# GpSimd takes three of the eight tiles of the residual update at two norm boundaries

## The chip, the cores and the metric

One core of one Trainium2 chip runs the whole program. The metric is the device time in microseconds, median over runs. The engines are named as in the profile: PE is TensorE, DVE is VectorE, ACT is ScalarE, POOL is GpSimd and SP is SyncE.

## The reference

Two hybrid transformer layers run one behind the other on 256 positions of 1024 features. The part that matters here is the end of the mixer and the end of the feed-forward block in the first layer:

```
x = x + gt1 * rmsnorm(mix, mix_post_g)
h = rmsnorm(x, ffn_pre_g) * (1.0 + sc2) + sh2
...
x = x + gt2 * rmsnorm(f, ffn_post_g)
h = rms_norm(x, attn_norm_2) * (1.0 + scale_a) + shift_a     # layer two
```

Here rmsnorm(v, g) is v * rsqrt(mean(v * v) + 1e-6) * g, the mean going over the 1024 features. So each boundary holds two norms in a row: one over the block's output, and, once x is updated, one over x.

## The kernel before

Features lie on the partitions: X is 128 x 8 x 256, eight tiles of 128 features by 256 positions, all float32. Linear layers run on TensorE as three products of high and low parts. ScalarE copies each weight chunk of 128 x 1024 from `ring` to its high part `WH` and GpSimd subtracts it from the original to get the low part `WL` (L505; the helper `low`, called by `lows` for a range of chunks). There are four slots, and a chunk's split waits until ScalarE has done the high part, which waits until the slot is free. Each engine has one instruction queue, in an order written out by hand, and semaphores tie the queues together.

A boundary goes like this. The last linear layer of the block leaves eight tiles in PSUM. ScalarE writes each to MIX (first boundary) or FO (second), scaled by gain and gate (L1414), and squares it (L1413). VectorE adds up the squares, TensorE sums them over the partitions, and `stat_root` on ScalarE makes the inverse root, RS[:, 0, :] (L1144, L1146; a table load stands between the two activations). Then `add_normed` on VectorE updates X: in three pairs of tiles and two single ones it multiplies the source by RS (L2052, 512 or 256 columns) into a slot of CT, waits for that with `st.link`, and adds it to X (L2053), which counts up `x_ready`. `square_x` on ScalarE waits for those counts and squares X into SQ (L1430) by the list SPANS, which counts up `sq_ready`. TensorE sums the eight squares with a matrix of ones as they come (`stat`), ScalarE makes the second inverse root, RS[:, 1, :], and `make_h` on VectorE with `make_hh` on ScalarE gives the high and low parts of h (L1791, L1187, L1796), tile by tile. TensorE's next linear layer begins with the first tile of h. While TensorE waits it runs `fill`: short products whose result is not used, ahead of each wait.

X is updated twice more in layer two, on VectorE alone (L2407), and SP stores it at the end. All wait on counts of `x_ready`.

GpSimd's queue is one call of `lows` from the middle of the first layer to the projection `o2` of the second; before it stand 16 products of the first layer's branch (L532).

Of the kernel before, what the change touches and what calls it, by code (L numbers as in the profile page):

```python
# [14 lines left out]
P = 128  # L15
T = 256
D = 1024
KD = D // P
FF = 2816
KF = FF // P  # L20
# [15 lines left out]
SLOTS = 4  # L36
# [46 lines left out]
PLAN = Stream()  # L83
# [33 lines left out]
SCRATCH = {}  # L117
# [9 lines left out]

OUT_Y, OUT_NSA, OUT_MLA = 0, 16, 24
SQ_O1, SQ_DOWN1 = 5, 21

ADA_AT = {}
for _n in range(8):
# [11 lines left out]
PAIR_END = PAIR_Q + HEADS1 // 2  # L144
# [27 lines left out]
def build(nc, x_t, par_in, ada_w, wts, out_t):  # L172
    F32, F32R, BF16 = mybir.dt.float32, mybir.dt.float32r, mybir.dt.bfloat16
    ALU, ACT, AX = mybir.AluOpType, mybir.ActivationFunctionType, mybir.AxisListType
    MUL, ADD, SUB = ALU.mult, ALU.add, ALU.subtract
    ctx = ExitStack()
    with ctx:
# [3 lines left out]
        def sem(name):  # L181
            return ctx.enter_context(nc.semaphore(name))
# [12 lines left out]
        X = sb("X", [P, KD, T])  # L195
# [9 lines left out]
        RS = sb("RS", [P, 2, T])  # L205
# [49 lines left out]
        MIX = region(R, 4096, a=8, b=T)  # L255

        FAH, FAL = region(RR, 0, a=KF, b=T), region(RR, KF * T, a=KF, b=T)
        FO = region(R, 12288, a=8, b=T)
# [58 lines left out]
        rs_ready = sem("rs_ready")  # L317
# [6 lines left out]
        fall_ready = sem("fall_ready")  # L324
        diff_ready, decay_ready, m_ready, m_used = sem("diff"), sem("decay"), sem("m_ready"), sem("m_used")
        y_ready, yn_ready, mixin_ready = sem("y_ready"), sem("yn_ready"), sem("mixin_ready")
        x_ready = sem("x_ready")
        lead_ready, evac_done = sem("lead_ready"), sem("evac_done")
        t_ready, hh_ready = sem("t_ready"), sem("hh_ready")
        wdt_hi, wdt_ready = sem("wdt_hi"), sem("wdt_ready")  # L330
# [3 lines left out]
        f_begun, f_conv, f_silu, f_act = sem("f_begun"), sem("f_conv"), sem("f_silu"), sem("f_act")  # L334
# [55 lines left out]
        def _(sp):  # L390
# [81 lines left out]
            uq, ukv, o2 = (PLAN.at[name][0] for name in ("uq", "ukv", "o2"))  # L472
            assert ukv + 4 == o2
            while c < CHUNKS:
# [4 lines left out]
                n = 0  # L479
# [10 lines left out]
                    load(c)  # L490
                    c += 1
            for j in range(KD):
                sp.wait_ge(x_ready, 3 * KD + j + 1)
                sp.dma_start(out_t[:, j * T:(j + 1) * T], X[:, j, :]).then_inc(out_sem, 16)
            sp.wait_ge(out_sem, 16 * KD)

# [1 line left out]
        @block.gpsimd  # L498
        def _(pool):
            def low(q, i=0):  # L500

                pool.wait_ge(hi_done, q + 1 + i * SLOTS)
                n = PLAN.cols[PLAN.chunk_of[q]]
                k = q % SLOTS
                nc.gpsimd.tensor_tensor(WL[:, k, 0:n], ring[:, k, 0:n], WH[:, k, 0:n].bitcast(F32), SUB  # L505
                                        ).then_inc(lo_done, 1)

            def lows(q, last):

                while q < last:  # L510
                    n = 0
                    while q + n < last and PLAN.cols[PLAN.chunk_of[q + n]] == PLAN.cols[PLAN.chunk_of[q]]:
                        n += 1
                    rounds = n // SLOTS
                    if rounds >= 2:
                        with pool.Fori(0, rounds, 1) as i:
                            for k in range(SLOTS):
                                low(q + k, i)
                        q += rounds * SLOTS
                    else:  # L520
                        low(q)
                        q += 1

            G = nc.gpsimd
            st = Steps(pool, pool_step)

            lows(0, PAIR_Q)

            for j in range(HEADS1 // 2):
                n = OUT_Y + j  # L530
                pool.wait_ge(o_free[n % 2], n // 2 + 1)
                G.tensor_tensor(Z[:, j, :], XBC[:, j, :], Z[:, j, :], MUL).then_inc(y_ready, 1)  # L532
            pool.wait_ge(lo_done, PAIR_END)
            lows(PAIR_END, PLAN.q("o2"))


            pool.wait_ge(mla_sq, 1)
            pool.wait_ge(cp_ready, 1)
            pool.wait_ge(kb_ready, 1)
            for t in range(2):  # L540
                k3 = KB[:, t, :].rearrange("p (h d) -> p h d", d=QK)
                rs = mlars[:, 16 * t + 8:16 * t + 16].unsqueeze(2)
                G.tensor_tensor(k3[:, :, 0:HD], k3[:, :, 0:HD], rs.to_broadcast([P, 8, HD]), MUL).then_inc(kb_scaled, 1)  # L543
                G.tensor_tensor(k3[:, :, HD:QK], KR[:, t, :].unsqueeze(1).to_broadcast([P, 8, ROPE]),
                                rs.to_broadcast([P, 8, ROPE]), MUL).then_inc(kb_scaled, 1)

            lows(PLAN.q("o2"), SPLITS)
# [3 lines left out]
        def _(pe):  # L551
# [120 lines left out]
            def stat(name, squares, n, i=0, base=None):  # L672
                out = scratch(name, i)
                for k in range(n):
                    stat_block(out, k, n, squares, base)
# [112 lines left out]
            for i in range(8):  # L788
                t, q = divmod(i, 4)
# [14 lines left out]
            for p in range(HEADS1 // 2 + 1):  # L804
                if p < HEADS1 // 2:
                    unit(PLAN.at["in1"][1] + 64 + p, PLAN.q("in1") + 64 + p, 1, h_hi, h_lo)
                if p >= 1:
                    n = p - 1
# [4 lines left out]
                    for t in range(2):  # L813
                        for e in range(2):
                            rows = slice(64 * e, 64 * e + 64)
                            cols = slice(P * n + 64 * e, P * n + 64 * e + 64)
                            m = SM[:, n % 2, 384 * e + t * 256:384 * e + t * P + 256]
# [19 lines left out]
            fill(u0, 6)  # L837
            pe.wait_ge(rs_ready, 6)
            fill(u0, 5)
            stat("stat_ffn1", sq_at, 8, base=13)  # L840
            fill(u0, 6)
            pe.wait_ge(rs_ready, 7)
            fill(u0, 4)
# [6 lines left out]
            fill(u0, 6)  # L850
            pe.wait_ge(rs_ready, 8)
            fill(u0, 5)
            stat("stat_attn", sq_at, 8, base=29)
            fill(u0, 6)
            pe.wait_ge(rs_ready, 9)
            fill(u0, 4)
# [17 lines left out]
            for c in range(1, 9):  # L874
                for t in range(2):
                    bank_wait(u0 + 2 * c + t)
                for part in range(2):
# [4 lines left out]
                    for t in range(2):  # L882
                        out = psL[:, (u0 + 2 * c + t) % 4, 0:256]
                        for b in range(4):
                            k = 4 * part + b
# [250 lines left out]
        def _(act):  # L1136
# [282 lines left out]
                    if m == 6:  # L1419
                        preload()  # L1420

            SPANS = ((0, 2), (2, 2), (4, 2), (6, 1), (7, 1))

            def square_x(base, sq_free_after):

                preload()
                act.wait_ge(s_done, sq_free_after + 1)
                for j, n in SPANS:
                    act.wait_ge(x_ready, base + j + n)
                    A(SQ[:, j * T:(j + n) * T], X[:, j:j + n, :].rearrange("p a b -> p (a b)"), ACT.Square).then_inc(sq_ready, n)  # L1430

            for n in range(2):
                act.wait_ge(s_free[n], (SCRATCH["stat_o1"] + 1 - n) // 2)
            scale_and_square("o1", MIX, lead[:, 8:16], 0, SQ_O1)
            stat_root("stat_o1", D, RS[:, 0, :])
            square_x(0, SCRATCH["stat_o1"])
            stat_root("stat_ffn1", D, RS[:, 1, :])
            make_hh(mod[:, 24:32], 8)

# [62 lines left out]
            act.wait_ge(f_act, KF)  # L1502
            scale_and_square("down1", FO, lead[:, 24:32], 1, SQ_DOWN1)
            stat_root("stat_down1", D, RS[:, 0, :])
            square_x(8, SCRATCH["stat_down1"])
            stat_root("stat_attn", D, RS[:, 1, :])
            make_hh(mod[:, 0:8], 16)
            u0 = PLAN.at["tok2"][1]
# [217 lines left out]
            def square_o2(m):  # L1726

                if m >= 1:
                    act.wait_ge(x_ready, 16 + m)
                    A(square_place(m - 1, 2), X[:, m - 1, :], ACT.Square).then_inc(sq_ready, 1)  # L1730

            act.wait_ge(s_done, SCRATCH["mla_p"] + 8)
# [19 lines left out]
        def _(dve):  # L1752
# [290 lines left out]
            def add_normed(src, rs, x_base):  # L2043

                def wide(buf, j, n):
                    return buf[:, j:j + n, :]

                for j, n, slot in ((0, 2, 0), (2, 2, 2), (4, 2, 0), (6, 1, 2), (7, 1, 3)):
                    t = CT[:, slot:slot + n, :]
                    if j >= 4:  # L2050
                        dve.wait_ge(x_ready, x_base + j - 2)
                    st.link(V.tensor_tensor(t, wide(src, j, n), rs.unsqueeze(1).to_broadcast([P, n, T]), MUL))  # L2052
                    V.tensor_tensor(wide(X, j, n), wide(X, j, n), t, ADD).then_inc(x_ready, n)  # L2053

            for m in range(8):
                add_squares(m, 5)
# [2 lines left out]
            dve.wait_ge(mixin_ready, 8)  # L2059
            dve.wait_ge(rs_ready, 6)  # L2060
            dve.wait_ge(evac_done, 8)
            add_normed(MIX, RS[:, 0, :], 0)
            dve.wait_ge(x_ready, 8)
            dve.wait_ge(rs_ready, 7)
            make_h(mod[:, 24:32], lead[:, 16:24], RS[:, 1, :], 8)

# [76 lines left out]
            dve.wait_ge(rs_ready, 8)  # L2143
            dve.wait_ge(f_act, KF)
            dve.wait_ge(evac_done, 16)
            add_normed(FO, RS[:, 0, :], 8)


            dve.wait_ge(x_ready, 16)
            dve.wait_ge(rs_ready, 9)  # L2150
            make_h(mod[:, 0:8], lead[:, 0:8], RS[:, 1, :], 16)

# [408 lines left out]
```

## Time and profile before

| | us |
|---|---|
| median of 3 runs | 1059.93 |
| lowest and highest | 1059.37, 1061.55 |
| span of the profiled execution | 1056.5 |
| median of the runs less that span | 3.4 |
| TensorE busy in it | 1025.1 (97%) |
| VectorE busy in it | 556.2 (53%) |
| ScalarE busy in it | 634.4 (60%) |
| GpSimd busy in it | 689.8 (65%) |

The span runs from the first to the last instruction of one profiled execution; the time of a run also holds what lies around it. No time of a run is given for the profiled execution itself, so the median of the runs stands beside its span. A busy share is an average over all stages, and a TensorE that runs filler products counts as busy.

### The profile page before, as it was taken

The page shows a single profiled execution, that of the slowest core. Times are in us where ns is not written, and L with a number is a line of the kernel's source. Part 1 is how long each engine was busy: PE and PEld are TensorE (multiplying, and loading weights), DVE is VectorE, ACT ScalarE, POOL GpSimd, SP SyncE. Part 2 cuts the span into 40 slices and gives each one's busy share as a digit, 9 for nine tenths or more (in the row PEclk, how much of TensorE's full clock was granted, in tenths as well). Part 3 has the DMA queues.
Part 4 walks back from the last instruction along what each step waited for, and adds up shares of the span by engine and source line. Part 5 has one row for each costly group of instructions (what it writes and reads, how often), then busy time and mean ns, then how long its engine had stood idle before and what let it go on. Part 6 is the DMA issues. An engine that isn't in the chain of part 4 may idle for free.

```text
span 1056.5 us, 23232 instructions
## 1 busy us (share of the span) xinstructions
PE 1025.1 (97%) x8537; PEld 966.4 (91%) x8537; DVE 556.2 (53%) x1165; ACT 634.4 (60%) x1133; POOL 689.8 (65%) x306
## 2 busy tenths in 40 slices
PE   7999999999999989999999899999989999999998
PEld 5999999988799979999999799998667699999998
DVE  2577625579874435565522542296566735444400
ACT  4555764477774576666645656744566557666642
POOL 2598899811269855988799287790031075988795
PEclk9999999999999999999999999999999999999999
DMA  9988888655547863777687289865201043665563
GB/s 380 383 306 282 273 307 298 235 191 187 174 146 259 282 236 105 273 235 248 204 279 268 80 283 360 330 239 191 99 21 60 1 140 122 217 193 189 168 217 111
DMA packets 62616, 226.43 MB, mean 214 GB/s; under 512 B 6960, under 2 KB 8272, under 8 KB 61264
## 3 DMA queue, kind: packets, MB, share of 16 engines
q1 hardware_dynamic: 61344, 221.23, 60.5%
q10 hardware_dynamic: 1200, 4.23, 1.4%
q8 instruction: 46, 0.75, 0.3%
q14 instruction: 26, 0.21, 0.1%
HBM read 224.35 MB, written 1.08 MB: 213 GB/s over the span
## 4 chain that ended last, share of the span: by engine, by line
PE 75%; issue 9%; POOL 9%; DVE 3%; ACT 3%; DMA 1%; POOLq 0%; ACTq 0%; DVEq 0%; SPq 0%
PE psL L553 68%; POOL WL L505 8%; PE psO L553 3%; PE psS L553 2%; PE psL L1092 1%; DMA ring<-wts 1%; ACT psL L1685 0%; ACT WH L1155 0%; ACT R L1273 0%; PE psS L1036 0%; ACT L1146 0%; DVE sm L2288 0%; PE psS L1063 0%; PE psS L966 0%; DVE CT L2052 0%
## 5 line engine op out<-in xcount | busy, mean ns | idle before, releaser
L505 POOL TENSOR_TENSOR WL<-ring,WH 128x1024 fp32r<-128x1024 f32 (+1 forms) x282 | 670.4, 2399 | 239.8 <-ACT WH L1155 186.7
L553 PE MATMUL psL<-HR,WH 128*128 128x256 f32 (+1 forms) x3096 | 513.5, 278 | 1.8 <-DVE HR L1796 0.9
L553 PEld LDWEIGHTS psL<-HR,WH 128*128 128x128 f32 (+1 forms) x3096 | 452.6, 187 | 7.5 <-issue 4.8
L553 PE MATMUL psL<-HR,WL 128*128 128x256 f32 x1536 | 396.2, 276 | 0.0
L1155 ACT ACTIVATE WH<-ring 128x1024 fp32r<-128x1024 f32 (+1 forms) x210 | 216.5, 1042 | 107.8 <-PE psL L553 71.9
L553 PEld LDWEIGHTS psL<-HR,WL 128*128 128x128 f32 x1536 | 275.2, 188 | 0.0
L553 PE MATMUL psL<-RR,WH 128*128 128x256 f32 x1356 | 205.2, 277 | 2.4 <-DVE RR L1981 1.2
L553 PEld LDWEIGHTS psL<-RR,WH 128*128 128x128 f32 x1356 | 185.5, 187 | 3.8 <-issue 2.8
L553 PE MATMUL psL<-RR,WL 128*128 128x256 f32 x672 | 145.0, 277 | 0.3 <-POOL WL L505 0.3
L2080 DVE SCALAR_TENSOR_TENSOR CT<-psL,par,CT 128x254 f32<-128x254 f32 (+1 forms) x176 | 80.9, 480 | 107.1 <-ACT CT L1463 102.0
L1454 ACT ACTIVATE WH<-ring 128x1024 fp32r<-128x1024 f32 (+1 forms) x88 | 92.9, 1058 | 71.4 <-PE psL L553 68.0
L1783 DVE SCALAR_TENSOR_TENSOR adaring<-adaring,psO 128x1024 f32<-128x1024 f32 x80 | 96.9, 1217 | 70.6 <-DMA adaring<-ada_w 66.5
L553 PEld LDWEIGHTS psL<-RR,WL 128*128 128x128 f32 x672 | 107.6, 188 | 0.6 <-POOL WL L505 0.5
L532 POOL TENSOR_TENSOR R<-R 128x256 f32<-128x256 f32 x16 | 13.4, 839 | 59.5 <-DVE R L1920 59.5
L1463 ACT ACTIVATE CT<-psL,par 128x256 f32<-128x256 f32 x88 | 48.2, 548 | 6.2 <-PE psL L553 6.2
L553 PE MATMUL psL<-WH,HR 128*128 128x256 f32 (+1 forms) x294 | 50.4, 278 | 0.7 <-DVE HR L1796 0.7
L553 PEld LDWEIGHTS psL<-WH,HR 128*128 128x128 f32 (+1 forms) x294 | 44.4, 186 | 1.0 <-issue 0.9
L1835 DVE SCALAR_TENSOR_TENSOR R<-psL,par,R 128x255 f32 (+2 forms) x72 | 34.7, 481 | 16.5 <-DVE R L1835 14.3
L543 POOL TENSOR_TENSOR R<-R,mlars 128x1024 f32<-128x1024 f32 x2 | 3.8, 1895 | 57.5 <-DVEq L2324 57.5
L2038 DVE TENSOR_TENSOR CT<-CT,psS 128x256 f32<-128x256 f32 x21 | 8.8, 421 | 60.6 <-ACT psS L1413 55.8
L553 PE MATMUL psL<-WL,HR 128*128 128x256 f32 x144 | 39.8, 276 | 0.0
L2407 DVE SCALAR_TENSOR_TENSOR X<-psL,mod,X 128x256 f32<-128x256 f32 x16 | 7.7, 484 | 59.0 <-PE psL L553 58.8
(274 smaller groups left out, 1122.8 us busy)
## 6 DMA issues: line engine op xcount, KB each, us to landing
ring<-wts SPq DMA_DIRECT2D x285, 512.0 KB, 4.2
adaring<-ada_w SPq DMA_DIRECT2D x80, 512.0 KB, 4.8
R<-ada_w SPq DMA_DIRECT2D x8, 1024.0 KB, 16.2
ring<-wts SPq DMA_DIRECT2D x16, 384.0 KB, 3.8
R<-cum_dram ACTq DMA_DIRECT2D x8, 512.0 KB, 4.1
R<-wts SPq DMA_DIRECT2D x8, 512.0 KB, 6.4
ring<-wts SPq DMA_DIRECT2D x8, 288.0 KB, 2.8
adaring<-wts SPq DMA_DIRECT2D x4, 512.0 KB, 5.2
```

What stands on the lines that cost most here:

```text
L505: nc.gpsimd.tensor_tensor(WL[:, k, 0:n], ring[:, k, 0:n], WH[:, k, 0:n].bitcast(F32), SUB).then_inc(lo_done, 1)
L532: G.tensor_tensor(Z[:, j, :], XBC[:, j, :], Z[:, j, :], MUL).then_inc(y_ready, 1)
L553: return nc.tensor.matmul(out, lhsT, rhs, start=start, stop=stop)
L1092: last = nc.tensor.transpose(out[0:wd, n * P:(n + 1) * P], src[:, t, o:o + wd], pv("ident"))
L1155: A(WH[:, k, 0:n], ring[:, k, 0:n], ACT.Copy).then_inc(hi_done, 1)
L1454: A(WH[:, q % SLOTS, 0:n], ring[:, q % SLOTS, 0:n], ACT.Copy).then_inc(hi_done, 1)
L1463: A(CT[:, 2 * slot + b, :], psL[:, u % 4, 0:T], ACT.Identity, scale=par[:, bass.ds(w0 + 2 * 44 + b * KF + j + it, 1)], bias=par[:, bass.ds ...
L1783: V.scalar_tensor_tensor(w, w, 1.0, cond, MUL, MUL, accum_out=col).then_inc(ada_used, 1)
L1835: ins = V.scalar_tensor_tensor(dst, psL[:, (u0 + k) % 4, 0:T - back], par[:, bass.ds(m + (c_w + (3 - back) * NXBC), 1)], dst, MUL, ADD)
L2038: ins = V.tensor_tensor(SUMS, SUMS, psS[:, m % 2, 0:T], ADD).then_inc(sq_added, 1)
L2080: ins = V.scalar_tensor_tensor(dst, psL[:, us[b] % 4, 0:T - back], par[:, bass.ds(w0 + (2 - back) * 44 + b * KF + j + it, 1)], dst, MUL, ADD)
L2407: V.scalar_tensor_tensor(X[:, m, :], lin(u), gates[:, m:m + 1], X[:, m, :], MUL, ADD).then_inc(lin_free[u % 4], 1)
```

## The change

`add_normed` on VectorE ends after tile 4: pairs (0, 1) and (2, 3), and tile 4 alone. GpSimd's queue gets `add_normed_tail`: tiles (6, 7) as a pair, then tile 5, each with a multiplication in place in the source tile and an addition to X that counts up the new semaphore `xpool_ready`. `square_x` takes the tiles in the order (0, 1), (6, 7), (2, 3), 4, 5, and TensorE sums the squares in that order. VectorE waits for GpSimd's tiles before it makes h. GpSimd's one call of `lows` becomes three, with a tail after the fourth chunk of `up1` and after the fourth of `tok2`. The counts of `x_ready` are named, since VectorE now counts 5 tiles and not 8 at these two boundaries.

```diff
+X_O1, X_DOWN1, X_O2, X_OUT = 0, 5, 10, 18
...
             pool.wait_ge(lo_done, PAIR_END)
-            lows(PAIR_END, PLAN.q("o2"))
+
+            def add_normed_tail(src, rs, use):
+
+                pool.wait_ge(rs_ready, 6 + 2 * use)
+                pool.wait_ge(evac_done, 8 * (use + 1))
+                for j, n in ((6, 2), (5, 1)):
+                    t, x = src[:, j:j + n, :], X[:, j:j + n, :]
+                    st.link(G.tensor_tensor(t, t, rs.unsqueeze(1).to_broadcast([P, n, T]), MUL))
+                    G.tensor_tensor(x, x, t, ADD).then_inc(xpool_ready, n)
+
+            lows(PAIR_END, PLAN.q("up1") + SLOTS)
+            pool.wait_ge(mixin_ready, 8)
+            add_normed_tail(MIX, RS[:, 0, :], 0)
+            lows(PLAN.q("up1") + SLOTS, PLAN.q("tok2") + SLOTS)
+            pool.wait_ge(f_act, KF)
+            add_normed_tail(FO, RS[:, 0, :], 1)
+            lows(PLAN.q("tok2") + SLOTS, PLAN.q("o2"))
...
-            stat("stat_ffn1", sq_at, 8, base=13)
+            stat("stat_ffn1", lambda k: sq_at((0, 1, 6, 7, 2, 3, 4, 5)[k]), 8, base=13)
...
-            stat("stat_attn", sq_at, 8, base=29)
+            stat("stat_attn", lambda k: sq_at((0, 1, 6, 7, 2, 3, 4, 5)[k]), 8, base=29)
...
-            SPANS = ((0, 2), (2, 2), (4, 2), (6, 1), (7, 1))
+            SPANS = ((0, 2, x_ready, 2), (6, 2, xpool_ready, 2), (2, 2, x_ready, 4), (4, 1, x_ready, 5), (5, 1, xpool_ready, 3))
...
-                for j, n in SPANS:
-                    act.wait_ge(x_ready, base + j + n)
+                for j, n, done_by, count in SPANS:
+                    act.wait_ge(done_by, count + (base if done_by is x_ready else 0 if base == X_O1 else 3))
...
-                for j, n, slot in ((0, 2, 0), (2, 2, 2), (4, 2, 0), (6, 1, 2), (7, 1, 3)):
+                for j, n, slot in ((0, 2, 0), (2, 2, 2), (4, 1, 0)):
...
+                dve.wait_ge(xpool_ready, 3 if x_base == X_O1 else 6)
```

## Rows read from the trace of the kernel before

**Rows 1.** The page's busy line: busy us, share of the span, instructions.
```profile
PE 1025.1 (97%) x8537; PEld 966.4 (91%) x8537; DVE 556.2 (53%) x1165; ACT 634.4 (60%) x1133; POOL 689.8 (65%) x306
```

**Rows 2.** Chain of waits, whole span: start us, us, what.
```profile
391.44 2.03 PE psS L553 x8
...
397.42 173.33 PE psL L553 x1524
...
584.95 5.39 PE psS L553 x16
```

**Rows 3.** Timeline, first boundary: start us, us, engine, line, form, idle before and releaser.
```profile
384.18 2.35 POOL L505 TENSOR_TENSOR WL<-ring,WH 128x1024 fp32r<-128x1024 f32 x1 [1.11 <-ACT WH L1155]
...
386.28 0.79 DVE L2052 TENSOR_TENSOR CT<-R,RS 128x512 f32<-128x512 f32 x1 [3.28 <-ACT RS L1146]
...
387.18 0.69 DVE L2053 TENSOR_TENSOR X<-X,CT 128x512 f32<-128x512 f32 x1
...
387.99 0.63 ACT L1430 ACTIVATE SQ<-X 128x512 f32<-128x512 f32 x1 [0.28 <-DVE X L2053]
...
388.77 1.10 PE L553 MATMUL psS<-SQ,par 128*128 128x256 f32 x4 [1.14 <-ACT SQ L1430]
...
391.83 0.42 DVE L2053 TENSOR_TENSOR X<-X,CT 128x256 f32<-128x256 f32 x1
392.30 0.42 ACT L1430 ACTIVATE SQ<-X 128x256 f32<-128x256 f32 x1 [0.38 <-DVE X L2053]
...
397.42 0.50 PE L553 MATMUL psL<-HR,WH 128*128 128x256 f32 x2 [0.50 <-DVE HR L1796]
```

**Rows 4.** Timeline, second boundary.
```profile
582.42 0.85 DVE L2052 TENSOR_TENSOR CT<-R,RS 128x512 f32<-128x512 f32 x1 [1.96 <-ACT RS L1146]
...
584.95 5.38 PE L553 MATMUL psS<-SQ,par 128*128 128x256 f32 x16 [1.13 <-ACT SQ L1430]
...
588.49 0.42 ACT L1430 ACTIVATE SQ<-X 128x256 f32<-128x256 f32 x1 [0.38 <-DVE X L2053]
```

**Rows 5.** Busy time by window: window, us; per engine; granted clock, DMA share, GB/s.
```profile
386.20:392.72 6.52, 4.89 (x24) 3.61 (x24) 5.59 (x10) 4.21 (x7) 0.33 (x1) 1.00 0.48 165
...
582.40:588.91 6.51, 5.34 (x21) 4.27 (x22) 5.65 (x10) 4.21 (x7) 0.32 (x1) 0.74 0.59 223
```

**Rows 6.** One line each: instructions, ns min/median/max, first and last start.
```profile
L2052 DVE TENSOR_TENSOR CT<-R,RS x10: 419/684/849, 386.3 to 587.6; 128x512 f32<-128x512 f32 x6, 128x256 f32<-128x256 f32 x4
...
L532 POOL TENSOR_TENSOR R<-R x16: 727/776/1645, 228.3 to 284.0; 128x256 f32<-128x256 f32 x16
...
L544 POOL TENSOR_TENSOR R<-R,mlars x2: 1042/1042/1043, 770.8 to 773.7; 128x512 f32<-128x512 f32 x2
```

**Rows 7.** Timeline, 691 to 708 us: splits and VectorE's instructions on two SBUF tiles.
```profile
691.48 2.59 POOL L505 TENSOR_TENSOR WL<-ring,WH 128x1024 fp32r<-128x1024 f32 x1
...
694.02 2.59 POOL L505 TENSOR_TENSOR WL<-ring,WH 128x1024 fp32r<-128x1024 f32 x1
694.27 2.62 DVE L2195 SCALAR_TENSOR_TENSOR R<-R,par,RS 128x256 f32<-128x256 f32 x1
...
702.46 2.85 POOL L505 TENSOR_TENSOR WL<-ring,WH 128x1024 fp32r<-128x1024 f32 x1
...
705.28 2.85 POOL L505 TENSOR_TENSOR WL<-ring,WH 128x1024 fp32r<-128x1024 f32 x1
```

**Rows 8.** Timeline, 284.5 us.
```profile
283.87 1.22 DVE L1926 TENSOR_TENSOR WL<-ring,WH 128x1024 fp32r<-128x1024 f32 x1
284.04 1.65 POOL L532 TENSOR_TENSOR R<-R 128x256 f32<-128x256 f32 x1 [0.42 <-DVE R L1920]
```

**Rows 9.** Timeline, 676 us: a split beside an instruction that reads PSUM (psO).
```profile
675.79 2.41 POOL L505 TENSOR_TENSOR WL<-ring,WH 128x1024 fp32r<-128x1024 f32 x1
...
675.92 1.22 DVE L1783 SCALAR_TENSOR_TENSOR adaring<-adaring,psO 128x1024 f32<-128x1024 f32 x1 [4.65 <-DMA adaring<-ada_w]
```

**Rows 10.** Timeline, GpSimd, 400 to 410 us.
```profile
407.08 4.78 POOL L505 TENSOR_TENSOR WL<-ring,WH 128x1024 fp32r<-128x1024 f32 x2 [20.55 <-ACT WH L1454]
```

More of the change, by code:

```diff
@@ L326, in build @@
         y_ready, yn_ready, mixin_ready = sem("y_ready"), sem("yn_ready"), sem("mixin_ready")
-        x_ready = sem("x_ready")
+        x_ready, xpool_ready = sem("x_ready"), sem("xpool_ready")
         lead_ready, evac_done = sem("lead_ready"), sem("evac_done")
@@ L492, in _ @@
             for j in range(KD):
-                sp.wait_ge(x_ready, 3 * KD + j + 1)
+                sp.wait_ge(x_ready, X_OUT + j + 1)
                 sp.dma_start(out_t[:, j * T:(j + 1) * T], X[:, j, :]).then_inc(out_sem, 16)
@@ L1435, in _ @@
             stat_root("stat_o1", D, RS[:, 0, :])
-            square_x(0, SCRATCH["stat_o1"])
+            square_x(X_O1, SCRATCH["stat_o1"])
             stat_root("stat_ffn1", D, RS[:, 1, :])
@@ L1504, in _ @@
             stat_root("stat_down1", D, RS[:, 0, :])
-            square_x(8, SCRATCH["stat_down1"])
+            square_x(X_DOWN1, SCRATCH["stat_down1"])
             stat_root("stat_attn", D, RS[:, 1, :])
@@ L1728, in square_o2 @@
                 if m >= 1:
-                    act.wait_ge(x_ready, 16 + m)
+                    act.wait_ge(x_ready, X_O2 + m)
                     A(square_place(m - 1, 2), X[:, m - 1, :], ACT.Square).then_inc(sq_ready, 1)
@@ L2061, in _ @@
             dve.wait_ge(evac_done, 8)
-            add_normed(MIX, RS[:, 0, :], 0)
-            dve.wait_ge(x_ready, 8)
+            add_normed(MIX, RS[:, 0, :], X_O1)
+            dve.wait_ge(x_ready, X_DOWN1)
             dve.wait_ge(rs_ready, 7)
@@ L2145, in _ @@
             dve.wait_ge(evac_done, 16)
-            add_normed(FO, RS[:, 0, :], 8)
-            dve.wait_ge(x_ready, 16)
+            add_normed(FO, RS[:, 0, :], X_DOWN1)
+            dve.wait_ge(x_ready, X_O2)
             dve.wait_ge(rs_ready, 9)
```

## The prediction

> **What bounds the kernel now.** I read the page's busy line first. TensorE is busy 97% of 1056.5 us and GpSimd 65% [rows 1], so GpSimd has time to give over the whole span, but a share of the span says nothing about one stage. So next the chain of waits around the two boundaries of layer one. At the first it leaves TensorE's linear products, goes through VectorE (the normed value, then X), ScalarE (squares), eight square sums on TensorE, the root on ScalarE, and comes back to the products at 397.42 [rows 2]. All of it is a serial stretch in which TensorE does only filler products. A microsecond saved or lost there moves everything behind it, because TensorE runs for 173 us without a gap from 397.42 on. The timeline of the stretch gives each link's length [rows 3], and the second boundary has the same shape 196 us later [rows 4].
>
> VectorE works from 386.28 to 391.83 + 0.42 = 392.25; the last square runs from 392.30 to 392.72 and the square sums end at 391.44 + 2.03 = 393.47, 0.75 after the last square [rows 2, 3]. At the second boundary the last square ends at 588.49 + 0.42 = 588.91, but the sums end at 584.95 + 5.39 = 590.34, 1.43 after it [rows 2, 4]. The granted TensorE clock explains the difference: 1.00 in the first stretch of updates, 0.74 in the second, so part of the second ran at 1.2 GHz and not 2.4 [rows 5]. Just before, TensorE had idled for 1.13 us ahead of its first square sum, between short groups of filler [rows 4]. That fall costs 1.43 - 0.75 = 0.68 us.
>
> **What the change removes and adds.** At each boundary VectorE keeps two pairs and one single tile, six instructions. A 512-column pair (0.68 + 0.69) and a 256-column single (2 x 0.42) go: 2.21 us [rows 3, 6]. GpSimd gets four new instructions: two of 512 columns and two of 256. If both engines ran freely beside each other, X would be complete about 1.2 us earlier (worked out as rival A). GpSimd has the time: its last weight split before the boundary ends at 384.18 + 2.35 = 386.53, and the next starts at 407.08 after 20.55 us of idleness [rows 3, 10]; after the second boundary TensorE starts its products in the same way, so I take the same gap. So the splits are delayed by nothing, the added waits on GpSimd's queue hold back no split that could run, and moving the tail between two loops of splits costs nothing. If that cover were gone, 4 us of tail would delay the weights by up to that. SP's queue sees only renamed counts. VectorE's new wait for GpSimd comes after its own last addition, where only the root was waited for anyway.
>
> **The two engines do not run freely beside each other.** Look at a stretch where GpSimd has splits queued and VectorE has instructions that read two SBUF tiles [rows 7]. A 256-column VectorE instruction takes 2.62 us in it. A 256-column addition to X takes 0.42 [rows 3]. And GpSimd's 1024-column split takes 2.59 instead of 2.35. They strictly take turns: one split, one VectorE instruction, and so on. With 256 columns between, the splits start 694.02 - 691.48 = 2.54 us apart; with 512 columns 705.28 - 702.46 = 2.82. It works the other way too: a 256-column GpSimd multiplication that began while VectorE had a 1024-column one took 1.65 us where the median is 0.776 [rows 6, 8]. And it depends on the operands: a VectorE instruction that reads one operand from PSUM takes 1.22 us with a split running beside it at 2.41, neither much delayed [rows 9]. All ten updates of X at a boundary read two SBUF tiles, and the four of GpSimd too. Even in the present kernel the very first one shows it: 0.79 (0.85 at the second boundary) where the median of its line is 0.684, because the last split was still running [rows 3, 4, 6].
>
> Now the price. From the two spacings 256 more columns cost 0.28, so VectorE holds its turn 0.28 for 256 columns and 0.56 for 512, and a 1024-column split holds it 2.54 - 0.28 = 2.26, 0.09 less than its 2.35. GpSimd's 512 columns have no row of this form. Between 0.776 for 256 and 2.35 for 1024, 256 columns are worth 0.52, so 1.30 for 512 and 0.69 for 256 when 0.09 is off each: turns of 1.21 and 0.69. The bounds are 1.04 from the one 512-column GpSimd form that the trace has, whose second operand is one repeated value [rows 6], and 1.30 plus nothing given back. I take 1.21, since these operands are like the split's.
> All turns together: VectorE 4 x 0.56 + 2 x 0.28 = 2.80, GpSimd 2 x 1.21 + 2 x 0.69 = 3.80, sum 6.60. They start at 386.39 (0.10 is lost to the last split, as now). In order: VectorE's first multiplication to 387.0; GpSimd's, waiting since 386.6, gets in while VectorE waits for its own result; then alternately. The first pair of X is complete at about 388.8 instead of 387.87 [rows 3], GpSimd's pair at 390.0, the second pair at 391.7, GpSimd's single tile at 392.4, and VectorE's single one, with 0.25 between its two instructions and after the second, at 386.39 + 6.60 + 0.25 = 393.24, where all of X was complete at 392.25. ScalarE then has two single squares to do one behind the other, where only one was left before: 393.28 to 394.02. Last square 394.02 - 392.72 = **1.30 us later**, at each boundary. Lower bound 0.68 (GpSimd's turns 0.95 and 0.64, by the shorter form and the shortest of 256 columns, 0.727), upper bound 2.4 (every instruction holds its turn for its whole duration: 3.6 + 4.1 = 7.7 instead of 6.6).
>
> The Trainium skill has a rule for this, on the page "SBUF — State Buffer", section "Who interferes with whom": a VectorE instruction with two SBUF inputs and a GpSimd instruction that reads SBUF share a port pair, and the second to start blocks until the first is wholly done. Rows 7 agree that one blocks and give a shorter turn: 2.82 for a 512-column instruction and a split, where the whole durations would be 2.35 + 0.69 = 3.04. By the rule to the letter the change would cost the upper bound, 4.8 us over both boundaries; by the rows it is 2.6.
>
> The clock comes on top. At the second boundary the square sums ended late because half of them ran at the lower clock; later squares shift them by 1.3 if the fall stays where it is, and by 1.30 - 0.68 = 0.62 if it goes. At the first boundary TensorE's idle time ahead of the first sum, 1.14 now [rows 3], grows by the 0.9 that the first pair is late. The second boundary fell at 1.13 of it in such a pattern while the first did not, so with 2.0 at both a fall is likelier: I take half of 0.68 for the first and keep the fall at the second. Sum: 1.30 + 0.34 + 1.30 = 2.94. Behind the boundaries nothing takes it back, since what follows, root, H and the products, is in the same chain. The profiled execution's span is 1056.5; the median of the runs, 1059.93, lies 3.4 above it, which I take as what lies around the span and leave alone. 1059.93 + 2.94 = **1062.9 us**.
>
> **Rivals.**
> (A) The engines do run side by side. Then GpSimd's pair is there at 386.6 + 2 x 1.30 + 0.1 = 389.3, its single at 391.0, squares end at 391.5: 1.2 us earlier at each boundary, 1057.5. For it: GpSimd is idle for 20 us and a share of 65%. Against: rows 7 and 8, on just this kind of operands. It decides where the two engines' spans may overlap in full, with no instruction longer than alone.
> (B) They take turns, but the turns are short and the clock does not fall: 2 x 0.68, with the second boundary's fall kept, 1061.3; 1060.6 with that fall gone. For it: the 1.04 form, and the clock's fall in one boundary out of two.
> (C) Turns for the whole duration, or the clock falls while the last sums run at both boundaries: 2 x 2.4 + 0.7 = 5.5 at most, 1065.4. For it: the rule above and the clock's fall at the second boundary. Against: the spacings in rows 7. It decides from the point where GpSimd's 512-column instruction holds its turn for over 1.6 us.
> (D) Nothing arrives: the shift is hidden by a weight load or a split that is late anyway. Against it: the first product's wait ends with VectorE's H, not with a weight [rows 3], and a run of 173 us of products follows [rows 2]. 1059.9.
>
> **How the numbers follow.** Forecast 0.58, A 0.05, B 0.20, C 0.12, D 0.05. The measurement tells some 0.2% (2.1 us) from no change: faster is below 1057.8, slower above 1062.05. A is faster. B and D are the same, and so is 0.07 of the forecast's 0.58, since 2.94 is only 0.8 above the bound and three runs of one kernel spread over 2.2 us; C is slower. That makes faster 0.05, same 0.32, slower 0.63. Range 1060.3 to 1065.4: from B's lower value less a little for the median to C's end.
>
> **What will show it.** Right: at both boundaries VectorE's second instruction (X of the first pair) takes about 1.6 us instead of 0.69, VectorE's spans are stretched wherever GpSimd's tail instructions are queued, GpSimd's second 512-column one takes 1.5 us and more, X is complete near 393.2 in this trace's time, the last square ends 1.3 later, and the root follows. Wrong: VectorE's six instructions at 0.68, 0.69 and 0.42 beside GpSimd's four (A); a last square under 0.7 later (B). A granted clock of 1.00 at both boundaries would take 0.3 to 1.0 off. GpSimd's splits starting later than 20 us after the boundary by more than the shift would show a cost that I put at nothing.

## The result and the profile after

| | us |
|---|---|
| before, median of 8 runs | 1058.79 (1055.78 to 1061.55) |
| after, median of 8 runs | 1062.13 (1060.16 to 1064.39) |
| ratio | 1.0033, 95% interval 1.0019 to 1.0048 |
| profiled execution: span, time | 1058.8, 1060.70 |

The change costs 3.5 us by the ratio; 2.94 was forecast. The median of before moved down by 1.1 us with more runs, so the forecast of 1062.9 stands 0.8 above the measured 1062.13. Of the executions timed for this document two (1152.52 us in before_filler2 and 2068.99 us in psum_late_table) lie far above the rest of their kernels and enter no ratio and no mean.

Below is the first boundary in the timeline of the changed kernel, which answers to [rows 3] (start us, us, engine, line, form). L2069 is VectorE's multiplication, L2070 its addition to X, L542 and L543 GpSimd's.

```profile
387.08 0.79 DVE L2069 TENSOR_TENSOR CT<-R,RS 128x512 f32<-128x512 f32 x1 [3.27 <-ACT RS L1163]
387.29 1.71 POOL L542 TENSOR_TENSOR R<-R,RS 128x512 f32<-128x512 f32 x1
...
387.98 1.57 DVE L2070 TENSOR_TENSOR X<-X,CT 128x512 f32<-128x512 f32 x1
...
389.14 1.53 POOL L543 TENSOR_TENSOR X<-X,R 128x512 f32<-128x512 f32 x1
389.47 1.75 DVE L2069 TENSOR_TENSOR CT<-R,RS 128x512 f32<-128x512 f32 x1
...
390.63 1.17 POOL L542 TENSOR_TENSOR R<-R,RS 128x256 f32<-128x256 f32 x1
...
391.32 1.03 DVE L2070 TENSOR_TENSOR X<-X,CT 128x512 f32<-128x512 f32 x1
391.88 1.05 POOL L543 TENSOR_TENSOR X<-X,R 128x256 f32<-128x256 f32 x1
392.28 0.94 DVE L2069 TENSOR_TENSOR CT<-R,RS 128x256 f32<-128x256 f32 x1
...
393.25 0.43 DVE L2070 TENSOR_TENSOR X<-X,CT 128x256 f32<-128x256 f32 x1
393.71 0.72 ACT L1447 ACTIVATE SQ<-X 128x256 f32<-128x256 f32 x2 [0.64 <-DVE X L2070]
```

Read down the two engines' lines: they alternate. VectorE's second instruction takes 1.57 us where it took 0.69, its third 1.75, its fourth 1.03, its fifth 0.94; only the last, with GpSimd done, is back at 0.43. VectorE does 2.2 us of work less and ends at 393.68, 6.60 us after its start where it was 5.98. Two single squares remain then, and the last ends at 394.43, 7.35 after the start instead of 6.44: **0.91 us later**.

Then TensorE, in the chain of waits of the changed kernel (start us, us, what), which answers to [rows 2]:

```profile
390.44 6.42 PE psS L570 x16
396.86 0.02 issue
396.89 0.47 ACT RS L1161
```

and in its busy time by window (window, us; PE, PEld, DVE, ACT, POOL; granted clock, DMA share, GB/s), which answers to [rows 5]:

```profile
386.20:394.00 7.80, 4.94 (x19) 4.06 (x20) 6.35 (x6) 4.45 (x8) 6.51 (x5) 0.69 0.44 164
394.00:401.00 7.00, 5.51 (x30) 4.67 (x29) 1.59 (x4) 3.52 (x7) 0.00 (x0) 0.86 0.00 1
585.30:592.00 6.70, 4.04 (x20) 3.04 (x21) 6.38 (x6) 3.42 (x6) 5.77 (x5) 1.00 0.54 211
592.00:598.00 6.00, 4.31 (x28) 3.52 (x27) 1.80 (x6) 3.80 (x7) 0.00 (x0) 1.00 0.00 1
```

The square sums ran for 6.42 us and ended 2.43 us after the last square; at full clock it was 0.75. The granted clock was 0.69 and 0.86 in the two windows: it had fallen from 2.4 to 1.2 GHz for most of the sums (over the sums alone it is 0.57). At the second boundary the clock stayed at 1.00 this time:

```profile
588.79 2.14 PE L570 MATMUL psS<-SQ,par 128*128 128x256 f32 x8 [2.01 <-ACT SQ L1447]
...
591.48 2.18 PE L570 MATMUL psS<-SQ,par 128*128 128x256 f32 x8 [0.56 <-ACT SQ L1447]
591.60 0.42 DVE L2070 TENSOR_TENSOR X<-X,CT 128x256 f32<-128x256 f32 x1
592.06 0.72 ACT L1447 ACTIVATE SQ<-X 128x256 f32<-128x256 f32 x2 [0.63 <-DVE X L2070]
```

There the last square ends 592.78 - 585.38 = 7.40 after VectorE's start (6.49 before), the sums 0.88 after it. The 2.01 in the first row is TensorE's idle time ahead of its first sum, 1.13 before [rows 4].

From VectorE's start to the end of the sums the two boundaries together took 9.78 + 8.28 = 18.06 us, against 7.19 + 7.92 = 15.11 before. That is 2.95 more in this pair of executions.

The next split of GpSimd after the first boundary, which answers to [rows 10]:

```profile
410.21 2.41 POOL L506 TENSOR_TENSOR WL<-ring,WH 128x1024 fp32r<-128x1024 f32 x1 [17.28 <-ACT WH L1471]
```

It waited 17.28 us for ScalarE, with the tail long done, and started 9.38 us after the first product at 400.83; before it was 407.08 - 397.42 = 9.66. At the second boundary it is 605.93 - 597.85 = 8.08 against 602.58 - 594.49 = 8.09.

### The profile page after: what moved, and what is told of

Same layout as the page of the kernel before. It is cut to its first block, busy times and chain, and to the rows that moved or that the text cites. A ratio compares the mean times of both kernels' runs of the same rounds, so it can differ in the third digit from the quotient of the medians.

```text
span 1058.8 us, 23229 instructions
## 1 busy us (share of the span) xinstructions
PE 1027.0 (97%) x8537; PEld 968.3 (91%) x8537; DVE 555.7 (52%) x1157; ACT 634.1 (60%) x1133; POOL 699.7 (66%) x314
## 4 chain that ended last, share of the span: by engine, by line
PE 83%; issue 6%; POOL 4%; DVE 3%; ACT 3%; ACTq 0%; POOLq 0%; DVEq 0%
PE psL L570 76%; POOL WL L506 4%; PE psO L570 3%; PE psS L570 3%; PE psL L1109 1%; ACT psL L1702 1%; ACT R L1290 0%; DVE X L2070 0%; ACT L1163 0%; DVE sm L2306 0%; DVE CT L2069 0%; ACT WH L1172 0%; PE psS L983 0%; PE psS L1053 0%; ACT R L1717 0%
```

## The experiments

Ratios are to the kernel before, run on the same chip in the same hours. The sets of runs were timed on different chips, so ratios of different kernels are compared no closer than their intervals. "Clock" is the granted TensorE clock, mean over a kernel's runs: 0.9966 for before (35 runs), 0.9934 after (8). From VectorE's first multiplication after the first root, one profiled execution of each kernel gave, in us (X complete and last square at the first boundary; the root is the second one, RS[:, 1, :]):

| kernel | X complete | last square | end of second root, at 1st / 2nd boundary | clock of runs | ratio (95%) |
|---|---|---|---|---|---|
| before | 5.98 | 6.44 | 9.42 / 10.15 | 0.9966 | |
| after | 6.60 | 7.35 | 12.00 / 10.52 | 0.9934 | 1.0033 (1.0019 to 1.0048) |
| first_only, 1st boundary | 6.60 | 7.35 | 10.98 / 9.47 | 0.9948 | 1.0028 (1.0011 to 1.0045) |
| after_filler | 6.60 | 7.36 | 10.47 / 10.53 | 0.9963 | 1.0026 (1.0013 to 1.0039) |
| after_filler2 | 6.60 | 7.36 | 10.48 / 10.54 | 0.9971 | 1.0034 (1.0018 to 1.0050) |
| before_filler | 5.97 | 6.42 | 9.42 / 9.47 | 0.9972 | 0.9992 (0.9976 to 1.0009) |
| before_filler2 | 5.97 | 6.42 | 9.42 / 9.47 | 0.9968 | 1.0006 (0.9993 to 1.0019) |
| one_tile | 6.05 | 6.59 | 11.40 / 11.48 | 0.9938 | 1.0035 (1.0021 to 1.0048) |
| beside_read | 8.78 | 9.23 | 13.84 / 12.81 | one run | one run |
| beside_write | 5.97 | 6.42 | 10.10 / 9.47 | one run | one run |
| psum | 4.56 (VectorE 3.68) | 5.02 | 8.94 / 8.99 | 0.9965 | 1.0007 (0.9992 to 1.0022) |
| psum_filler | 4.56 (VectorE 3.68) | 5.01 | 8.94 / 9.00 | 0.9973 | 0.9975 (0.9963 to 0.9988) |
| psum_filler8 | 4.57 (VectorE 3.68) | 5.02 | 8.95 / 9.00 | 0.9972 | 0.9991 (0.9978 to 1.0004) |
| psum_late_table | 4.56 (VectorE 3.68) | 5.60 | 9.62 / 9.61 | 0.9971 | 1.0003 (0.9991 to 1.0015) |

My theory: the engines take turns on instructions that read two SBUF tiles (1), and the later squares leave TensorE idle so that its clock falls (2). Rivals: GpSimd hinders VectorE through shared tiles and semaphores or by any work on SBUF; the clock costs nothing; the loss lies in the splits.

**Turn-taking: the tail's shapes beside an unchanged VectorE.** Added to the kernel before, on an unused part of R (so the views call it R too), with GpSimd's splits in three loops as in the change:

```diff
+                    st.link(G.tensor_tensor(t, t, rs.unsqueeze(1).to_broadcast([P, n, T]), MUL))
+                    st.link(G.tensor_tensor(x, x, t, ADD))
```

> The kernel before, VectorE updating all eight tiles, with the four GpSimd instructions of the change added on tiles that nobody uses (the same shapes, RS as the second operand). Turn-taking: the four turns of 1.2, 1.2, 0.7 and 0.7 us come between VectorE's ten instructions: X complete 9.3 to 9.8 us after the root instead of 6.0. Rival (GpSimd hinders only where the two share data, tiles or semaphores): 6.0.

Timeline of VectorE's first five instructions at the first boundary:

```profile
385.91 0.79 DVE L2070 TENSOR_TENSOR CT<-R,RS 128x512 f32<-128x512 f32 x1 [3.29 <-ACT RS L1164]
386.80 1.57 DVE L2071 TENSOR_TENSOR X<-X,CT 128x512 f32<-128x512 f32 x1
388.29 1.75 DVE L2070 TENSOR_TENSOR CT<-R,RS 128x512 f32<-128x512 f32 x1
390.14 1.03 DVE L2071 TENSOR_TENSOR X<-X,CT 128x512 f32<-128x512 f32 x1
391.09 1.21 DVE L2070 TENSOR_TENSOR CT<-R,RS 128x512 f32<-128x512 f32 x1
```

The same 1.57, 1.75 and 1.03, with no tile of VectorE's but RS shared and none of its semaphores. RS is not the cause either: VectorE's additions to X (1.57 and 1.03) do not read it. X is complete 8.78 - 5.98 = 2.80 us later for GpSimd's four instructions, 0.5 to 1.0 less than expected.

The other half takes the reads away:

```diff
+                for n in (4, 4, 2, 2):
+                    st.link(G.memset(IDLE[:, 0:n, :], 0.0))
```

> The same, but GpSimd's four instructions only write: memsets of 1024, 1024, 512 and 512 columns on the unused tiles, some 0.5 to 1.3 us each. If turns are taken because both engines read two SBUF tiles: VectorE's instructions stay at 0.69 and 0.42, X complete 6.0 us after the root. Rival (any GpSimd work on SBUF costs VectorE its turn): X complete 8 us or more after the root.

```profile
387.93 3.12 POOL L542 MEMSET R<- 128x1024 f32 x4
```

```profile
388.64 0.69 DVE L2069 TENSOR_TENSOR X<-X,CT 128x512 f32<-128x512 f32 x1
389.25 0.68 DVE L2068 TENSOR_TENSOR CT<-R,RS 128x512 f32<-128x512 f32 x1
390.04 0.69 DVE L2069 TENSOR_TENSOR X<-X,CT 128x512 f32<-128x512 f32 x1
```

GpSimd writes to SBUF for 3.12 us (first fence, its timeline) and VectorE's instructions beside it take what they take alone (second). It is GpSimd's reading that matters here, not its working. This kernel has the three loops of splits too, and its stages are those of before, with the fall of the clock at the first boundary and not at the second (10.10 and 9.47, where before has 9.42 and 10.15); so the loops cost nothing there.

**Turn-taking: VectorE's second operand out of SBUF.**

```diff
-            stat_root("stat_o1", D, RS[:, 0, :])
+            stat_root_twice("stat_o1", D, RSP["stat_o1"], RS[:, 0, :])
...
-                for j, n, slot in ((0, 2, 0), (2, 2, 2), (4, 1, 0)):
-                    t = CT[:, slot:slot + n, :]
+                for j, n, slot in ((0, 2, 1), (2, 2, 2), (4, 1, 3)):
+                    t = psL[:, slot, 0:n * T].rearrange("p (a b) -> p a b", b=T)
```

`stat_root_twice` writes the root to PSUM (`RSP`) for VectorE, then to SBUF for GpSimd.

> The changed kernel, but VectorE reads RS and its product from PSUM (ScalarE writes the root to a PSUM bank for VectorE and 0.4 us later to SBUF for GpSimd; the product goes to three free PSUM banks), so that none of VectorE's six instructions reads two SBUF tiles. Turn-taking by operands: VectorE's instructions take 0.69 and 0.42 again beside GpSimd's four, which take 1.3 and 0.8; X complete 4.7 us after the root instead of 6.6, last square 1.2 us earlier than before at each boundary, ratio 0.997 to 0.9985 (about 1056.4). Rival (the engines hinder each other whatever the operands, by memory bandwidth): instructions still 1.0 to 1.7 us long, ratio 1.003.

Timeline, first boundary:

```profile
387.20 0.69 DVE L2081 TENSOR_TENSOR psL<-R,psS 128x512 f32<-128x512 f32 x1 [3.25 <-ACT psS L1174]
...
387.58 1.27 POOL L545 TENSOR_TENSOR R<-R,RS 128x512 f32<-128x512 f32 x1
...
388.00 0.69 DVE L2082 TENSOR_TENSOR X<-X,psL 128x512 f32<-128x512 f32 x1
388.60 0.69 DVE L2081 TENSOR_TENSOR psL<-R,psS 128x512 f32<-128x512 f32 x1
388.76 0.20 ACT L1413 ACTIVATE sm<-eps_col 128x1 f32<-128x1 f32 x1
389.00 1.27 POOL L546 TENSOR_TENSOR X<-X,R 128x512 f32<-128x512 f32 x1
...
389.82 4.08 PE L573 MATMUL psS<-SQ,par 128*128 128x256 f32 x16 [1.28 <-ACT SQ L1459]
...
391.03 0.73 POOL L546 TENSOR_TENSOR X<-X,R 128x256 f32<-128x256 f32 x1
```

Same tiles, same split of the work: VectorE at 0.69 and GpSimd at 1.27 and 0.73, side by side. X is complete 4.56 us after the start (4.7 expected), and the last square comes 1.42 us earlier than before. But the root comes only 9.42 - 8.94 = 0.48 earlier. TensorE's 16 instructions of square sums last 4.08 us in a row and are now the bound, at a clock of 1.00; they end 1.69 after the last square, and begin only at 389.82, since ScalarE's small activation behind its table load, until 388.96, holds the first square. That is where the expected 1.2 us per boundary went. The ratio, 1.0007, lies above the expected 0.997 to 0.9985 and confirms no gain.

**How it grows with the tiles.** GpSimd takes tile 7 alone.

```diff
-                for j, n in ((6, 2), (5, 1)):
+                for j, n in ((7, 1),):
```

> GpSimd updates tile 7 alone, VectorE three pairs and tile 6. By turns: VectorE saves 0.8 us and gets two turns of 0.7 us put in, X complete 6.4 us after the root (6.0 before, 6.6 with three tiles), last square 0.4 us later than before at each boundary; total with the clock 0.5 to 2 us over before, ratio 1.0005 to 1.0018. Rival (the loss grows with the tiles only from some number on): X complete 5.2 to 5.6 us after the root, ratio 0.9985 to 0.9995.

```profile
391.94 1.10 PE L570 MATMUL psS<-SQ,par 128*128 128x256 f32 x4 [1.47 <-ACT SQ L1447]
393.75 4.53 PE L570 MATMUL psS<-SQ,par 128*128 128x256 f32 x12 [0.71 <-ACT SQ L1447]
```

X is complete 0.07 us later, not 0.4, and the last square 0.15: nearly nothing. Yet the time is 1.0035. The first pair of X came 0.33 later, TensorE idled 1.47 us ahead of its sums, and the clock fell at both boundaries: the last 12 of 16 sums took 4.53 us, and the root came 2.0 and 1.3 us late. The interval of its ratio begins at 1.0021, and my accounting gives 2.0 + 1.3 = 3.3 us (1.0031) for this execution; the mean clock, 0.9938, is as low as that of the whole change. So here the clock is all of the loss that I can place. The profiled execution was the slowest of the kernel's ten, though (1066.27 us, the median is 1063.39), so its two falls may be more than the usual.

**The clock.** The changed kernel with filler in TensorE's idle time ahead of the sums, then also behind them:

```diff
-            fill(u0, 5)
+            fill(u0, 12)
             stat("stat_ffn1", lambda k: sq_at((0, 1, 6, 7, 2, 3, 4, 5)[k]), 8, base=13)
-            fill(u0, 6)
+            fill(u0, 9)
```

The last pair of lines is in after_filler2 alone.

> The changed kernel with 12 instead of 5 filler products between the first root and the square sums, at both boundaries, so that TensorE idles 0.5 us there and not 2.0. If the granted clock falls because TensorE idles: clock 1.00 in both stretches, square sums end 0.8 us after the last square at both, 1.0 to 1.7 us less than the changed kernel (ratio to before 1.0015 to 1.0025); the last square itself does not move. If the fall has another cause: the clock still falls at a boundary, the added filler runs at half speed and pushes the sums back, and the ratio is 1.0033 or more.

```profile
386.38 2.94 PE L570 MATMUL psL<-par 128*128 128x128 f32 x24 [1.03 <-ACT RS L1163]
389.78 2.13 PE L570 MATMUL psS<-SQ,par 128*128 128x256 f32 x8 [0.45 <-ACT SQ L1447]
392.47 2.19 PE L570 MATMUL psS<-SQ,par 128*128 128x256 f32 x8 [0.56 <-ACT SQ L1447]
```

With TensorE idle for 0.45 us and not 2.0 the sums ran at full clock at both boundaries, and the roots came 1.53 us earlier and in the same place as at after's second boundary, where the clock had not fallen (10.47 and 10.53, after 10.52). But in this execution the clock fell a little later, from 595.9, in the linear products, where each pair then takes 0.63 instead of 0.39. The ratio, 1.0026 (1.0013 to 1.0039), does not tell the gain from none.

```profile
595.66 0.38 PE L570 MATMUL psL<-WH,HR 128*128 128x256 f32 x1 [0.74 <-DVE HR L1813]
595.85 0.40 PE L570 MATMUL psL<-WL,HR 128*128 128x256 f32 x1
596.05 0.63 PE L570 MATMUL psL<-WH,HR 128*128 128x256 f32 x2
```

> The changed kernel with 12 instead of 5 filler products ahead of the square sums and 9 instead of 6 behind them: the change without its cost in clock. By the later last square alone, 2 x 0.92 and 2 x 0.13 us: 2.1 us over before, ratio 1.0020; mean granted clock 0.996 or more. Rival (the clock costs nothing on the path, all of the 1.0033 is turn-taking): ratio 1.0033.

Its profile shows no fall at or behind either boundary. What is left in the stages is turn-taking alone: 10.48 + 10.54 - 9.42 - 9.47 = 2.13 us, 1.0020, inside its interval (1.0018 to 1.0050) but at its edge; the timing does not tell it from 1.0033. The mean clock of its runs, 0.9971, is as high as that of before, and its time is still that of the change. So the stages show the clock's part and the timing of this kernel does not confirm that filler gives it back.

> The kernel before with 9 instead of 5 filler products at the same two places, TensorE idling 0.2 us there instead of 1.1. Clock theory: the fall at the second boundary goes, sums end 0.75 us after the last square, 0.2 to 0.7 us less on average (ratio 0.9993 to 0.9998), too little for the timing alone. Rival: no change in the clock, ratio 1.0000 or above.

The fall in the second boundary's sums went in the profile (9.47 instead of 10.15), though here too the clock fell just behind, in the products (0.53 from 594.4 to 598). The timing shows no difference, as expected of so small a term.

> The kernel before with 9 instead of 5 filler products ahead of the square sums and 9 instead of 6 behind them. It tells what the filler alone is worth: if the clock costs the kernel before 0.3 to 1 us on average (mean granted clock of its runs 0.9966), ratio 0.999 to 0.9998. Rival (the gain of the kernel with PSUM operands and filler, 0.9975, is all filler, and GpSimd's tiles earn nothing): ratio 0.9975.

1.0006: filler alone earns nothing that can be timed, so a gain of the PSUM kernel with filler would not be the filler's.

Taken together, the fourteen profiled executions show how idle time and the fall go together. TensorE idled 1.13 to 2.01 us ahead of its first sum at 14 boundaries, and at 8 of them the granted clock over the sums was 0.57 to 0.73; it idled 0.15 to 0.61 us at the 14 others, and over all of their sums the clock was 1.00. But the idle time does not settle it: with 2.01 us at both of after's boundaries one fell and the other did not.

**One boundary.** The second as in before:

```diff
-            pool.wait_ge(f_act, KF)
-            add_normed_tail(FO, RS[:, 0, :], 1)
```

> GpSimd's tail stands at the first boundary alone; the second is as in the kernel before. Turn-taking and the clock (my theory): each boundary carries about half, so 1.3 to 2.6 us over the kernel before (ratio 1.0012 to 1.0025); in its trace VectorE needs 6.6 us from first multiplication to last addition at the first boundary and 6.0 at the second. Rival (one of the two boundaries carries all, or the loss lies in GpSimd's three loops of splits): ratio 1.0033 or 1.0000, with the two boundaries no different from before in VectorE's time.

VectorE's times were as expected (6.60 at the first, 6.03 at the second). The first boundary's root came 1.56 late, 1.07 of it from turns and 0.5 from a fall. The interval of the ratio, 1.0011 to 1.0045, is too wide to say whether a boundary carries half or more; its value, 1.0028, leans against half.

**A better version?** PSUM operands, with filler:

> The kernel with VectorE's operands in PSUM, and 10 instead of 5 filler products ahead of the square sums and 9 instead of 6 behind them. In that kernel the squares came 1.4 us earlier than before but TensorE, with 4.1 us of square sums from 2.6 us after the root on, gave back all but 0.5 us. If the clock is what took the rest away: no fall at either boundary or just behind it in most runs, mean granted clock 0.997 or more, 1 to 2 us less than before (ratio 0.998 to 0.999). Rival (the rest of the gain is lost elsewhere): ratio 1.0007 as without the filler.

> The kernel with PSUM operands and 8 and 9 filler products, ScalarE's table load ahead of the first square as it was. Against the one with the load put behind, whose last square came 0.6 us later, it tells what the place of the load costs; against the one with 10 and 9, whether its 0.9975 holds. By the stages, 2 x 0.5 us before the clock and the part of the clock's cost that the kernel before has: ratio 0.997 to 0.9990. Rival (0.9975 was chance, the stage gains nothing that can be timed): 1.0000 or more.

> The kernel with PSUM operands and filler (8 and 9), and ScalarE's early table load, which held its first square until 1.8 us after the root with X of the first pair done at 1.5, put behind the first square. Square sums start 0.25 us earlier and end 0.25 earlier, at both boundaries: 0.5 us less than that kernel (ratio 0.9970). Rival: the load then delays the second square and the root, ratio 0.9975 or more.

The two filler kernels differ by two filler products ahead of the sums, and their stages are those of psum (8.94 to 9.00), so filler gave nothing back there: what the stage had lost was TensorE's row of sums and not the clock. The intervals of their ratios, 0.9975 and 0.9991, overlap. With psum's 1.0007 their middle is 0.9991, which is what 2 x 0.48 us would give. Only one of the three is clear of 1, so a gain of about 1 us over before is what the stages give, and the timing does not settle it. Against the changed kernel both filler kernels are clear, by some 4 us or more. Moving the table load was a miss:

```profile
389.08 0.63 ACT L1458 ACTIVATE SQ<-X 128x512 f32<-128x512 f32 x1 [1.36 <-DVE X L2083]
389.73 1.28 ACT L1413 ACT_TABLE_LOAD   x1
391.02 0.20 ACT L1413 ACTIVATE sm<-eps_col 128x1 f32<-128x1 f32 x1
391.31 1.76 ACT L1458 ACTIVATE SQ<-X 128x512 f32<-128x512 f32 x4
```

The first square starts 1.61 after the root instead of 1.85, but the square of GpSimd's pair, which was complete 3.1 us after it, had to wait for the load till 3.8. TensorE idled for 1.04 us between its sums and the root came 0.67 later than in psum_filler8. The rival had it.

## Why the prediction was right, step by step

- **GpSimd has the time, the splits are not delayed.** Right: 9.38 us against 9.66 from the first product to the next split.
- **The engines take turns.** Right, shown four ways: the same stretched durations in beside_read, none with memsets, none with PSUM operands, and the alternation in the changed kernel. Durations stretch where GpSimd reads SBUF beside a VectorE instruction with two SBUF operands, and do not where either of the two is missing.
- **The price of a turn: too high.** The order was as forecast: in the time of the trace before (0.80 less than in the changed kernel's) X's first pair is complete at 388.75, GpSimd's pair at 389.87, the second pair at 391.55, GpSimd's single tile at 392.13 and VectorE's at 392.88, where I had 388.8, 390.0, 391.7, 392.4 and 393.24. X complete was 0.62 later and not 0.99, the last square 0.91 later and not 1.30. The term that was off is GpSimd's turns: I had 3.80 for four, beside_read shows 2.80. Part of it was made up by VectorE's own part, which I had too low: 2.80 of turns, 0.25 of waits and 0.10 at the start, 3.15 in all, where its own time is 5.98 - 2.21 = 3.77. And 3.77 + 2.80 = 6.57 is what was measured (6.60). GpSimd's durations alone were right (1.27 for the predicted 1.30, 0.73 for 0.78). But I priced its turn from the spacing of its own instructions, [rows 7], 0.09 under their duration. VectorE lost less than that in each: 2.62 - 0.48 = 2.14 beside a 2.35 split (an instruction of this form alone takes 0.485), and 1.57 - 0.69 = 0.88 beside GpSimd's 1.27. Why it is less at the boundary is not shown; each turn may begin in the 0.1 us in which VectorE waits for its own product.
- **Two squares at the end instead of one.** Right: 0.75 from X complete to the last square's end, 0.47 before.
- **The rule of the Trainium skill**, "SBUF — State Buffer", section "Who interferes with whom". By its blocking for the whole instruction I had put 2.4 us per boundary; measured 0.91. That one blocks the other is what the changed kernel and beside_read show, and the whole durations are too high a price for it: 7.7 us from first multiplication to X complete by them, 6.60 measured. The page says in the same place that a VectorE instruction with two SBUF inputs does not contend with a GpSimd instruction that only writes SBUF: the memsets agree, 5.97 us against 5.98.
- **The clock: too low, and not settled.** I had 0.34 on top. Over all runs the mean granted clock went from 0.9966 to 0.9934, 0.0032 of 1060 us or 3.4 us of full-speed time; how much of it falls into waits and costs nothing is not shown. The stages give the change 2.13 us where the clock does not fall, so of the 3.5 some 1.4 is left. That is a remainder and not a measurement of the clock: after_filler2, with a mean clock of 0.9971, still took 1.0034. In the profiled execution the clock took 1.5 at the first boundary, and at the second the 0.7 of before's fall did not recur.
- **The sum** came out 0.6 below the measured difference, and that it came so near is in part luck: 2.6 for 1.8 in the last squares, 0.34 for the 1.4 that is left over, and 0.3 that I had not seen (0.13 at each boundary because the last two squares reach TensorE together, 0.04 for VectorE's added wait).
- **What lies around the span.** I took 3.4 us from a median and another execution's span. In the profiled execution of after it is 1060.70 - 1058.8 = 1.9.

Open: why the timed ratios of first_only and of the filler versions of the change lie 0.6 to 1.5 us above what their stages add up to (1.56 and 2.13 us). The profiles differ outside the two stages: by up to 3 us in when the first boundary is reached (385.9 to 389.1), before anything that was changed, and by more behind the second. From the end of its root to the start of a run of 162 products of TensorE (850.35 in after's chain of waits) the profiled executions took 255.5 us in before and 254.5 in after, but 257.6 and 257.5 in the two filler versions of the change, 257.5 and 257.2 in those of before, and 256.3 in first_only. In this stretch the chain of waits can go through GpSimd's splits. In before it does:

```profile
699.13 12.35 POOL WL L505 x4
...
711.52 10.81 PE psL L553 x72
```

and in after it does not:

```profile
679.41 45.97 PE psL L570 x384
```

So the filler versions may lose here what they gain at the boundaries, and the prediction's sentence that nothing behind the boundaries takes the shift back is not shown. One execution of each kernel cannot settle either, and no kernel here was made to.

## What to carry to other kernels

Before moving half of an elementwise chain to a second engine, look for a place in the trace where the two already work at once on the same kinds of operands, and read the waiting engine's duration there; idle time on the helper says nothing about it. If they take turns, put one of VectorE's operands in PSUM before moving work (its instructions were back at 0.69 and 0.42 us here), and then ask what stands next in the chain: here TensorE's 4.1 us of sums kept two thirds of the gain. Where TensorE waits for the first result, look also at its granted clock in the work that follows, not just at when the last result comes: here it fell in some executions and at some boundaries, and that moved the root by 0.5 to 2 us.

## What I had not expected of the hardware

Moving a single tile of eight cost next to nothing up to the last update (X 0.07 us later) and 1.0035 in time, with the mean granted clock of the runs down from 0.9965 to 0.9938. TensorE's idle time ahead of its sums had gone from 1.14 to 1.47 us. Filler there raised the mean clock of the changed kernel from 0.9934 to 0.9963, but a fall could come later instead, after the short idle times around the second root, and then in the products themselves, and the time did not follow the mean clock: 1.0026 and 1.0034 with filler, 1.0033 without.
